# Delta-rule query roots and decays taken between the convolutions of a two-block kernel

## What the kernel computes

```
qkv = silu(causal_depthwise_conv(concat([qa, ka, va]), conv_w))   # 12 tiles of 128 channels
q, k = l2_normalize(q), l2_normalize(k)                           # 4 heads x 128
beta = sigmoid(ba)
g = -exp(a_log) * softplus(aa + dt_bias)                          # decays, 4 heads x 512
gc = cumsum(g) within chunks of 64
lmat = strict(k_beta @ k.T * exp(gc_i - gc_j))
tmat = inverse(I + lmat)                                          # by chunks
... a recurrence over 8 chunks ...
o = rms_norm(o) * silu(za)
```

## Time and profile before

| | |
|---|---|
| median of 3 runs | 1930.93 us (1930.76 to 1934.62) |
| the profiled execution's own time | 1929.69 us |
| its span | 1927.9 us |
| instructions | 25166 |
| TensorE's granted clock | 1.0 |
| PE busy | 1914.7 us, 99% |
| DVE busy | 1220.2 us, 63% |
| ACT busy | 935.2 us, 49% |
| POOL busy | 709.5 us, 37% |

### The profile page before, as it was taken

One profiled execution on the slowest core, in us unless ns is written; L12 is line 12 of the kernel. 1 busy time (PEld: TensorE's weight loads), 2 busy tenths in 40 slices (PEclk: granted clock), 3 DMA queues, 4 the chain that ended last, 5 costly groups with the idle time before them and its releaser, 6 DMA issues.

```text
span 1927.9 us, 25166 instructions
## 1 busy us (share of the span) xinstructions
PE 1914.7 (99%) x9658; PEld 1549.4 (80%) x9658; DVE 1220.2 (63%) x2106; ACT 935.2 (49%) x1433; POOL 709.5 (37%) x534
## 2 busy tenths in 40 slices
PE   9999999999999999999999999999999999999999
PEld 6878888877788878788877788777766788989989
DVE  6667756555745667766464737665544447878787
ACT  6455553343345465544334345587555445444343
POOL 5545432434355454432434455546222354000000
PEclk9999999999999999999999999999999999999999
DMA  5434542423535335632424545422211333323231
GB/s 203 129 114 133 141 137 72 165 71 116 196 104 173 99 115 148 163 102 70 163 69 137 184 142 154 160 87 85 72 55 55 117 102 119 113 75 121 87 110 66
DMA packets 94790, 227.70 MB, mean 118 GB/s; under 512 B 29936, under 2 KB 34032, under 8 KB 93360
## 3 DMA queue, kind: packets, MB, share of 16 engines
q1 hardware_dynamic: 88752, 222.95, 36.0%
q10 hardware_dynamic: 5920, 3.15, 0.6%
HBM read 193.95 MB, written 24.64 MB: 113 GB/s over the span
## 4 chain that ended last, share of the span: by engine, by line
PE 86%; DVE 9%; DMA 2%; ACT 1%; SPq 1%; issue 1%; POOL 1%; ACTq 0%; DVEq 0%
PE bank L466 84%; DVE kv L400 1%; DVE ER L400 1%; PE bank L470 1%; SPq L395 1%; DVE tmp L400 1%; DMA X<-inverses 1%; DVE scs L425 1%; DMA kv<-blocks 1%; DVE tmp L410 1%; DVE m8s L422 0%; DVE fl L400 0%; POOL wl L400 0%; DMA st<-units 0%; ACT wh L455 0%
## 5 line engine op out<-in xcount | busy, mean ns | idle before, releaser
L400 POOL TENSOR_TENSOR wl<-st,wh 128x512 fp32r<-128x512 f32 x490 | 660.4, 1371 | 850.3 <-ACT wh L455 850.2
L466 PE MATMUL bank<-hh,wh 128*128 128x512 f32 x1616 | 651.2, 404 | 1.9 <-ACT hh L452 0.7
L466 PE MATMUL bank<-hh,wl 128*128 128x512 f32 x1616 | 629.3, 390 | 0.0
L466 PE MATMUL bank<-hl,wh 128*128 128x512 f32 x1616 | 628.9, 390 | 0.0
L455 ACT ACTIVATE wh<-st 128x1024 fp32r<-128x1024 f32 (+1 forms) x302 | 316.9, 1050 | 170.3 <-PE bank L466 128.2
L466 PEld LDWEIGHTS bank<-hh,wh 128*128 128x128 f32 x1616 | 303.3, 188 | 88.6 <-issue 24.8
L466 PEld LDWEIGHTS bank<-hl,wh 128*128 128x128 f32 x1616 | 303.7, 188 | 67.0 <-issue 6.9
L466 PEld LDWEIGHTS bank<-hh,wl 128*128 128x128 f32 x1616 | 303.3, 188 | 64.8
L400 DVE TENSOR_TENSOR xt<-xt,bank 128x512 f32<-128x512 f32 x80 | 54.8, 686 | 115.7 <-PE bank L466 115.7
L466 PE MATMUL bank<-fh,wh 128*128 128x256 f32 x448 | 127.0, 284 | 0.7 <-DVE wl L400 0.7
L466 PE MATMUL bank<-fl,wh 128*128 128x256 f32 x448 | 126.8, 283 | 0.0
(11 more groups left out here) (363 smaller groups left out, 3016.6 us busy)
## 6 DMA issues: line engine op xcount, KB each, us to landing
st<-units SPq DMA_DIRECT2D x300, 512.0 KB, 3.5
gates<-tmp SPq DMA_DIRECT2D x48, 256.0 KB, 2.7
gt<-gates SPq DMA_DIRECT2D x48, 256.0 KB, 3.7
pads<-tmp SPq DMA_DIRECT2D x32, 128.0 KB, 2.9
qk<-tmp SPq DMA_DIRECT2D x16, 256.0 KB, 4.2
x_scratch<-xt SPq DMA_DIRECT2D x2, 2048.0 KB, 9.2
xt<-x_scratch SPq DMA_DIRECT2D x2, 2048.0 KB, 8.6
ph<-phi SPq DMA_DIRECT2D x8, 512.0 KB, 4.7
```

The lines of the kernel that those rows point to most:

```text
L400: return NOTHING if self.e is None else self.e.tensor_tensor(out, a, b, op)
L466: return NOTHING if self.e is None else self.e.matmul(out, lhsT, rhs, start=start, stop=stop, skip_group_check=share)
```

## The change

It moves the root of the query's norm and the decays from the first steps of `delta` into `front1`, and takes steps out of `delta`:

- PE makes the query's sums after convolution tile 8, in bank 0 instead of bank 4. The key's sums go to bank 2, "tp" and "gl" to bank 3, and they and the two `spread` calls lie closer together. Four steps ahead of the blocks are gone.
- ACT has `head_roots(l, 0, 0)` and the four decay instructions at convolution tile 9, and `head_roots(l, 1, 2)` at the start of `delta`.
- DVE has the query's `mixed` and the decays' first two instructions before the last operation of tile 10, the scan and `gx` before that of tile 11.
- POOL and SP wait four steps fewer ahead of their parts of `delta`.
- `SELECT`, the idle steps of the search ahead of its parts, goes from 8 to 5 in its first entry.

```diff
-SELECT = (8, 12, 3)
+SELECT = (5, 12, 3)
...
@@ PE front1
+                if c == 8:
+                    pe.wait_ge(*at("dn_sq", l, 0, 3))
+                    sums(0, layer[l].aa4, "dn", l, 0)
@@ PE delta
-            pe.wait_ge(*at("dn_sq", l, 0, 3))
-            sums(4, aa4, "dn", l, 0)
+            spread(L.mix[0], "dn", l, 0)
             pe.wait_ge(*at("dn_sq", l, 1, 3))
-            sums(5, L.aa4k, "dn", l, 1)
-            yield
-            yield
-            spread(L.mix[0], "dn", l, 0)
-            yield
-            spread(L.mix[1], "dn", l, 1)
-            yield
-            yield
-            o = bank(4, "tp", l)
+            sums(2, L.aa4k, "dn", l, 1)
+            o = bank(3, "tp", l)
...
             yield
-            o = bank(5, "gl", l)
-            pe.wait_ge(*at("free4", "tp", l))
+            o = bank(3, "gl", l)
...
+            yield
+            spread(L.mix[1], "dn", l, 1)
             yield
@@ ACT front1
+                if c == 9:
+                    head_roots(l, 0, 0)
+                    z1, z2 = L.Y
+                    ac.wait_ge(*at("small_v", l, 1))
+                    ac.act(z2[R1, :], z1[R1, :], ACT.Abs).then_inc(*sig("small_a", l, 1))
+                    ac.wait_ge(*at("small_a", l, 1))
+                    ac.act(z2[R1, :], z2[R1, :], ACT.Exp, -1.0).then_inc(*sig("small_a", l, 2))
...
@@ DVE front1
+                if c == 10:
+                    mixed(L.mix[0], L.aa4[0], "dn", l, 0)
...
+                if c == 11:
+                    dv.wait_ge(*at("small_v", l, 3))
+                    dv.scan(L.rw[R1, :], C("reset")[R1, :], z1[R1, :], 0.0).then_inc(*sig("small_v", l, 4))
...
@@ DVE delta
+            scaled(0)
             dv.wait_ge(*at("tp", l))
...
             yield
-            yield
-            yield
+            mixed(L.mix[1], aa4[1], "dn", l, 1)
             dv.wait_ge(*at("egl", l))
...
@@ POOL delta
-            yield from idle(8)
+            yield from idle(4)
@@ SP delta
-            yield from idle(10)
+            yield from idle(6)
```

More of the change, by code:

```diff
@@ L1045, in delta @@
         def delta(l):
-            L, aa4 = layer[l], layer[l].aa4
-            yield
-            pe.wait_ge(*at("dn_sq", l, 0, 3))
-            sums(4, aa4, "dn", l, 0)
-            pe.wait_ge(*at("dn_sq", l, 1, 3))
-            sums(5, L.aa4k, "dn", l, 1)
-            yield
+            L = layer[l]
             yield
             spread(L.mix[0], "dn", l, 0)
-            yield
-            spread(L.mix[1], "dn", l, 1)
-            yield
-            yield
-            o = bank(4, "tp", l)
+            pe.wait_ge(*at("dn_sq", l, 1, 3))
+            sums(2, L.aa4k, "dn", l, 1)
+            o = bank(3, "tp", l)
             pe.wait_ge(*at("small_v", l, 4))
@@ L1616, in gate, with head_roots @@
                 ac.act(tmp[g][:], banks[b][:], ACT.Tanh, 0.5, bias).then_inc(*sig(f"free{b}", "gate", l, j))
+        def head_roots(l, f, b):
+            L, aa4 = layer[l], layer[l].aa4
+            ac.wait_ge(*at("dn_mm", l, f))
+            rnorm(aa4[f][:], banks[b][:], b, ("dn", l, f), "dn_r", l, f)
+            ac.wait_ge(*at("dn_r", l, f))
+            ac.cp(L.mix[f][:], aa4[f][:]).then_inc(*sig("dn_hi", l, f))
         def front1(l):
@@ L1645, in front1 @@
                     ac.act((L.aa4, L.aa4k)[f][h][:], (L.qf, L.kf)[f][:, h, :], ACT.Square, 0.5).then_inc(*sig("dn_sq", l, f, h))
+                if c == 9:
[5 more added lines that the diff above has]
+                    ac.act(z2[R1, :], z2[R1, :], ACT.Exp, -1.0).then_inc(*sig("small_a", l, 2))
+                    ac.wait_ge(*at("small_a", l, 2))
+                    ac.act(z2[R1, :], z2[R1, :], ACT.Ln, 1.0, 1.0).then_inc(*sig("small_a", l, 3))
+                    ac.act(colx[R1, 0:1], K(f"alog{l}", 0, R1), ACT.Exp).then_inc(*sig("small_a", l, 4))
         def proj(l):
@@ L1688, in delta @@
         def delta(l):
-            L, aa4 = layer[l], layer[l].aa4
+            L = layer[l]
             ac.wait_ge(*at("hb2", l))
             yield
[L1692 to L1706, removed]
+            head_roots(l, 1, 2)
+            yield
             ac.wait_ge(*at("gl", l))
-            ac.act(L.egl[:].rearrange("p b c -> p (b c)"), banks[5][:, 0:16], ACT.Exp).then_inc(*sig("egl", l))
-            ac.wait_ge(*at("free5", "gl", l))
+            ac.act(L.egl[:].rearrange("p b c -> p (b c)"), banks[3][:, 0:16], ACT.Exp).then_inc(*sig("egl", l))
+            yield
+            ac.wait_ge(*at("free3", "gl", l))
             ac.act(L.gcol[:, 1, :, :], L.gcol[:, 1, :, :], ACT.Exp).then_inc(*sig("gexp", l, 0))
@@ L2256, in index, with mixed @@
             dv.tt(out, out, xs, ALU.add).then_inc(*sig(name, *key))
+        def mixed(mix, x, name, *key):
+            dv.wait_ge(*at(f"{name}_hi", *key))
+            dv.stt(mix[:], mix[:].bitcast(F32), C("later"), x[:], ALU.mult, ALU.subtract).then_inc(*sig(f"{name}_mix", *key))
         def front1(l):
@@ L2279, in small @@
                     index(L.ki[:], L.ik, L.iks, at("swapik", l, 4), "ki", l)
+                if c == 10:
+                    mixed(L.mix[0], L.aa4[0], "dn", l, 0)
+                    dv.wait_ge(*at("small_a", l, 3))
+                    dv.wait_ge(*at("small_v", l, 1))
+                    dv.stt(z1[R1, :], z1[R1, :], 0.0, z2[R1, :], ALU.max, ALU.add).then_inc(*sig("small_v", l, 2))
+                    dv.wait_ge(*at("small_a", l, 4))
+                    dv.wait_ge(*at("small_v", l, 2))
+                    dv.ts(z1[R1, :], z1[R1, :], colx[R1, 0:1], ALU.mult, -1.0, ALU.mult).then_inc(*sig("small_v", l, 3))
+                if c == 11:
+                    dv.wait_ge(*at("small_v", l, 3))
+                    dv.scan(L.rw[R1, :], C("reset")[R1, :], z1[R1, :], 0.0).then_inc(*sig("small_v", l, 4))
+                    dv.wait_ge(*at("small_v", l, 4))
+                    dv.cp(L.gx[R1, :], L.rw[R1, :]).then_inc(*sig("g_hi", l))
+                    dv.wait_ge(*at("g_hi", l))
+                    dv.stt(L.gx[R1, :], L.gx[R1, :].bitcast(F32), C("second")[R1, :], L.rw[R1, :], ALU.mult, ALU.subtract).then_inc(*sig("g_mix", l))
             for c in range(12):
@@ L2336, in delta, with scaled @@
             yield
-            for m in range(2):
-                mixed(L.mix[m], aa4[m], "dn", l, m)
-            for f in range(2):
-                yield
-                if f == 0:
-                    yield
+            def scaled(f):
                 dv.wait_ge(*at("dn_up", l, f))
@@ L2346, in delta @@
                     dv.stt(x, x, 0.5 * (1.0 if f else 128.0 ** -0.5), banks[4 + c][:], ALU.mult, ALU.mult).then_inc(*sig(f"free{4 + c}", "dn_row", l, f, c))
[L2347 to L2360, removed]
             gc, beta = L.tpc[:, 0, :, :], L.tpc[:, 1, :, :]
-            bv = f4(banks[4][:])
+            bv = f4(banks[3][:])
+            scaled(0)
             dv.wait_ge(*at("tp", l))
```

15 lines of the change are left out of this document (6 added, 9 removed).

## The result

The changed kernel takes 1971.42 us as the median of four runs (1966.27 to 1972.21), the kernel before 1931.86 us as the median of four (1930.76 to 1934.62): 1.0198 times as long, with a 95% interval of 1.0186 to 1.0210. The sign was forecast, the size was not: 14 us were, and 39.6 came by the medians (38.3 by the ratio).

What follows compares the result with a forecast made beforehand. PE, busy 99% of the span, was taken to bound the kernel. Terms of 4.3+0.95+1.15-0.5+1.15 = 7.05 us a layer, 14.1 for two, gave a median of 1945 us; range 1935.5 to 1952.

Steps and rivals of the forecast that it cites:

- The key's sums: First step of `delta`: PE waits 0.6 us for ACT's last square, which follows tanh of tile 11.
- The chunk-end matmul: In `delta`, "gl" on PE waits 1.0 us for copies that stand behind DVE's four scalings.
- The end of tile 11's taps: End of the convolutions on DVE: at 111.9 us, bounds 110.9 to 113.9, where it was 106.0 before.
- Part 4: Behind the front: bank 3 at the rows' mean costs 0.95 us a layer, the second head's `lT` 1.15.
- the last pair: Search's last products at the layer's end: both pairs back to back, some 2.0 us of waiting, 1.5 more than before.
- part 3: Key's spread: cast, POOL's low half and `swap0` make DVE's pair late; PE waits about 4.0 us.
- part 5: From the blocks on, all comes sooner: inverses' DMA wait goes, -0.5 us; tail of the layer +1.15, bounds 0.3 to 1.8.
- Rival D: Inverses' DMA becomes late behind a row's store on SP: some 2.5 us a layer, 1950; chance 0.08.
- Only the front is real: Rival A: part 4 fits into half tiles, the tail nets zero; 3.8 us or less a layer, 1936 to 1938.5; chance 0.16.
- The front holds: Rival B: the key's pair is ready in time and the gains stay, 2.6 us a layer, 1925.7; chance 0.07.
- The losses and gains cancel: Rival C: wait at the spread about 1.5 us, the rest hidden; 1927 to 1935; chance 0.08.
- Rival E: Table switches on ACT cost what the page says, load plus drain; 1950 on the sum; chance 0.03.

Runs made afterwards that it cites:

- e7: The kernel before with 16 small DVE copies ahead of the pair of the query's roots, making one long PE wait a layer; 1945.6 us, ratio 1.0072.
- e3: The changed kernel with four idle steps put back behind the key's spread on every engine and the search back at 8; 1950.3 us, ratio 1.0088.
- e6: The changed kernel with the search at 8 and four idle steps between the blocks and the inverses; 1957.1 us, ratio 1.0133.
- e1: The changed kernel with only the search's first idle count back at 8 from 5; 1964.5 us, ratio 1.0159.
- e5: e3 with DVE's pair of the key's roots also put ahead of the rotation of the index query; 1934.9 us, ratio 1.0015.
- e2: The changed kernel with DVE's pair of the key's roots put ahead of the rotation of the index query; 1969.9 us, ratio 1.0198.
- e8: The kernel before with 8 small DVE copies ahead of the pair of the query's roots, for a short PE wait; 1930.7 us, ratio 0.9997.
- e9: The kernel before with only the query's sums, root and pair moved between the convolutions, decays and `delta` steps left in place; 1932.7 us, ratio 1.0004.

## Why the prediction was wrong

**What held.** The waits at the front were forecast one by one. The key's sums: 0.6 forecast, 0.52 measured. The chunk-end matmul: 1.0 and 1.3. The end of tile 11's taps: 111.9 and 112.09. The table load without a drain: 1.28 at 97.61 with ACT going on at 98.90, so the drain that the Trainium skill, "ScalarE: Activation LUTs", section "What ACT_TABLE_LOAD costs", puts behind a switch isn't seen here either. Part 4's two collisions: 0.95 at the rows' mean and 1.15 for `lT`, measured 0.92 and 1.05; the places were read from the order, but the sizes were the middles of 0 to 1.9 and 0 to 2.0, so that they came this close was luck. The wait for `X` is gone, and the last pair waits, 1.56 where 2.0 was forecast.

**The step mis-sized: part 3, the wait at the key's spread.** 4.0 forecast, 5.8 measured. The mechanism was right, down to the queue. Two of its terms were too small. The rotation took 4.9 us, not the 2.85 of its upper bound, with POOL's second unit beside all of it. And the swap landed at 122.3, not 121.3: POOL's low half took 3.12 us and not 2.55, so the swap went out 0.7 later, and it took 0.2 longer to land. So the pair was ready 2.8 us later than summed; PE came to the spread 0.9 later (122.2 for 121.3), and the difference is the 1.8. With 1.3 for 1.0, the waits of the front less the 1.2 saved are 6.4 where 4.3 were summed.

**The step that failed: there was no term for the clock.** I costed a wait at its own length. e7 shows it for one wait a layer in an otherwise untouched kernel: the matmuls behind the waits of 6.2 and 5.8 cost 1.6 and 2.6 us more than before. Read in the same way, against the same rows of the kernel before, the wait at the key's spread costs 1.4 and 2.7 beyond its length in the changed kernel and 2.4 and 2.1 in e3. Four stretches of layer 0 in the changed kernel are like that, behind the waits of 5.8, 3.9, 2.4 and 1.6. The 42.3 us of span are 31.1 of waits (40.9 in all against 9.8) and 11.2 of the rest, the most of it this.

**The step that failed most: part 5, "what is won later".** It took all that comes sooner behind the blocks as gain, but for the last pair of products, and never asked what the search three steps sooner does. It has a net of +0.65 a layer (1.15 less 0.5), and the 0.5 did not come: the wait for the inverses' DMA is 1.1 us in both layers, against 0.9. Measured by the medians: 3.7 a layer for the inverses and the recurrence (e6 to e1) and 3.5 for the search (e1 to the changed kernel), 7.2 in all (6.3 by the ratios); in layer 0 of the profiled executions even 10.5. That DVE is nearly full where the inverses are stood in the profile of before (busy for 47.0 of the 50 us from 180 to 230); a row's operations queued there free ACT's buffer by way of a store, and PE's mean waits for ACT. Rival D had the queue (the store of a row behind late DVE operations) but at the wrong end of it, the inverses' DMA: that wait stayed at 0.4 to 0.8.

**The sum again**, a layer, by the medians: front 9.1 for 4.3, blocks 3.4 for 2.1, the rest 7.2 for 0.65, together 19.7 for 7.05. (0.95 of the 2.1 was the wait for bank 3, which goes with the search in e1; counted there, it is 3.4 for 1.15 and 7.2 for 1.6.)

**Rivals.** "Only the front is real" falls: e3 is 21 us under the changed kernel. "The front holds" falls in the changed kernel; e5 shows what it would have taken, room behind the spread and the pair ahead of the rotation, and even then it is 0.15% slower than before (1.0006 to 1.0025). "The losses and gains cancel" needed DVE through tile 11 by 109.5; it was 112.09. Rival E, the drain at a switch, falls too: none is seen.

**Open.** How the cost of the search splits between the layers was not taken apart: 7.9 in layer 0 and 5.2 in layer 1 of the profiled executions, of which e1's was its fastest, and 3.5 on the mean of both by the medians. Whether e2's edit would pay with the search alone at 8 was not run. That a row's swap holds `lT` back is read from the trace and was not tested by itself. Where the clock begins to fall stays open too, and the length of a wait alone doesn't settle it: behind a single wait of 1.7 us in layer 1 of e8 (at 815.6) it stayed at 1.00, behind a single one of 2.4 in layer 1 of e3 (at 833.1) it was 0.51 for 3.5 us, and behind one of 1.4 among small matmuls in e6 (at 172.4) it was 0.54 for 3.7 us.

## What to carry to other kernels

In a hand-woven program with one engine at 99%, every side engine's work between two uses by the busy one has slack in time behind it, and steps taken out of a side chain spend that slack. Removing idle steps and putting more work ahead of them in the same edit spends it twice: try one at a time (e9 was free and e5 cost 0.15%, the whole change 2%). When a wait is taken from one place, look for the next user of the same late engine before counting the gain (e2 gave 1.6 us of 14). A wait of TensorE of some us must be priced with the slower matmuls behind it, here 1.4 to 2.7 us for one of about 6. And for each step that is moved, walk the in-order queues that it is put into, down to the buffers freed by a store.

## What the runs showed of the hardware

One wait of 6.2 us of TensorE, in a kernel at a granted clock of 1.000 otherwise, brings the matmuls behind it to 1.2 GHz (0.43 us apart instead of 0.23) and costs 1.6 us beyond its length (e7, layer 0; 2.6 us behind the 5.8 of layer 1). Waits of 0.7 and 1.7 do not (e8), one of 2.4 does (e3, layer 1). The Trainium skill, "TensorE: Matmul & The Clock Gate", says in its section "Loop structure matters more than you think" that a long wait for DMA between matmuls lets the clock drop; the trace agrees, with the numbers above, and here the long wait was for DVE.

DVE's 128x512 operations on two SBUF tiles took 1.61 to 1.75 us with POOL's subtractions beside them (122.32 to 127.19) and 0.68 to 0.69 without (the same three operations of the next rotation, 131.23 to 133.2, where POOL has nothing under way). The Trainium skill, "GPSIMD Engine Reference", section "8. Key points", names contention between the two engines when DVE has two inputs in SBUF; the trace agrees, and here it was worth 2.9 us in the chain that PE waited for.
